# A triangular inverse whose diagonal blocks of 16 are solved row by row on VectorE, with packed gate products and folded square sums, in a one-core streaming-encoder layer

## The reference, cut to what matters

```python
L = jnp.where(strict, jnp.einsum('nbhtd,nbhsd->nbhts', kb, kc) * decay, 0.0)
T = lax.linalg.triangular_solve(L, eye, left_side=True, lower=True, unit_diagonal=True)
u = jnp.einsum('nbhts,nbhse->nbhte', T, vc * bc[..., None])
w = jnp.einsum('nbhts,nbhsd->nbhtd', T, kb * jnp.exp(G)[..., None])
```

```python
def rmsnorm(x, g):
    y = xf * lax.rsqrt(jnp.mean(xf * xf, axis=-1, keepdims=True) + EPS)
```

## Time and profile before

| | |
|---|---|
| time, median of 3 runs | 2031.48 us (2030.72 to 2032.32) |
| the profiled execution: its time, its span | 2031.48 us, 2029.6 us |
| granted clock of TensorE, mean | 0.998 |
| DVE, ACT, POOL busy | 1221.1 (60%), 898.0 (44%), 30.6 (2%) |
| DMA | 378.71 MB, mean 187 GB/s |

### The profile page before, as it was taken

The page is one execution under the profiler, slowest core; times in us unless marked ns, Lnnn a source line. Parts: engine busy times, 40 slices in busy tenths (PEclk is TensorE's granted clock), DMA queues, the critical chain, the costliest instruction groups (busy, mean ns, idle before and its releaser), DMA issues.

```text
span 2029.6 us, 35130 instructions
## 1 busy us (share of the span) xinstructions
PE 2014.8 (99%) x15008; PEld 1923.9 (95%) x15008; DVE 1221.1 (60%) x1330; ACT 898.0 (44%) x890; POOL 30.6 (2%) x53
## 2 busy tenths in 40 slices
PE   8999999999999999999999999999999999999999
PEld 8999999999999999999999999988888888888888
DVE  5677644544544467576564445778777777854444
ACT  5445333434365434454444434544444444433333
POOL 0000000000000000000000000000000000000000
PEclk9999999999999999999999999999999999999999
DMA  8565444555556856556565446655565656566664
GB/s 269 174 200 193 140 141 140 191 175 174 182 172 210 288 172 223 189 176 190 174 189 157 131 156 199 219 196 186 186 198 174 207 175 197 171 207 210 192 200 138
DMA packets 355454, 378.71 MB, mean 187 GB/s; under 512 B 8015, under 2 KB 351347, under 8 KB 353939
## 3 DMA queue, kind: packets, MB, share of 16 engines
q1 hardware_dynamic: 350947, 353.63, 54.7%
q0 software_dynamic: 4400, 23.48, 3.1%
HBM read 366.06 MB, written 11.02 MB: 186 GB/s over the span
## 4 chain that ended last, share of the span: by engine, by line
PE 97%; DMA 1%; DVE 1%; ACT 1%; issue 0%; SPq 0%; DVEq 0%; ACTq 0%
PE bank L1884 18%; PE bank L1885 18%; PE bank L1886 18%; PE bank L1921 16%; PE bank L1923 8%; PE bank L2395 8%; PE bank L2396 4%; PE bank L2078 1%; PE bank L2125 1%; DMA raw<-in_w_in 1%; PE bank L2303 1%; PE bank L2322 1%; DVE w_lo_home L1083 1%; ACT w_hi_home L496 0%; PE bank L2119 0%; PE bank L1989 0%
## 5 line engine op out<-in xcount | busy, mean ns | idle before, releaser
L1083 DVE TENSOR_TENSOR w_lo_home<-raw,w_hi_home 128x2048 fp32r<-128x2048 f32 (+1 forms) x349 | 756.8, 2169 | 602.4 <-ACT w_hi_home L496 602.0
L496 ACT ACTIVATE w_hi_home<-raw 128x2048 fp32r<-128x2048 f32 (+2 forms) x359 | 645.1, 1798 | 1071.6 <-PE bank L1886 639.3
L1884 PE MATMUL bank<-x_home,w_hi_home 128*128 128x256 f32 x2304 | 648.8, 282 | 2.2 <-DVE w_lo_home L1083 2.2
L1885 PE MATMUL bank<-x_home,w_hi_home 128*128 128x256 f32 x2304 | 643.6, 279 | 0.0
L1886 PE MATMUL bank<-x_home,w_lo_home 128*128 128x256 f32 x2304 | 642.9, 279 | 0.0
L1921 PE MATMUL bank<-x_home,w_hi_home 128*128 128x512 f32 x1408 | 488.5, 390 | 0.1
L1884 PEld LDWEIGHTS bank<-x_home,w_hi_home 128*128 128x128 f32 x2304 | 433.4, 188 | 3.0 <-issue 2.7
L1885 PEld LDWEIGHTS bank<-x_home,w_hi_home 128*128 128x128 f32 x2304 | 433.5, 188 | 0.2
L1886 PEld LDWEIGHTS bank<-x_home,w_lo_home 128*128 128x128 f32 x2304 | 433.2, 188 | 0.0
L1923 PE MATMUL bank<-x_home,w_lo_home 128*128 128x256 f32 x1408 | 397.0, 282 | 0.0
L1921 PEld LDWEIGHTS bank<-x_home,w_hi_home 128*128 128x128 f32 x1408 | 264.4, 188 | 55.7 <-issue 0.4
(11 more groups left out here) (301 smaller groups left out, 2003.7 us busy)
## 6 DMA issues: line engine op xcount, KB each, us to landing
raw<-in_w_in SPq DMA_DIRECT2D x52, 2048.0 KB, 8.7
raw<-in_ffn_up SPq DMA_DIRECT2D x44, 2048.0 KB, 8.0
raw<-in_ffn_down SPq DMA_DIRECT2D x32, 1408.0 KB, 6.5
raw<-in_xa_wkv SPq DMA_DIRECT2D x16, 2048.0 KB, 9.2
raw<-in_w_br SPq DMA_DIRECT2D x8, 2048.0 KB, 8.2
raw<-in_w_out SPq DMA_DIRECT2D x8, 2048.0 KB, 8.2
raw<-in_xa_wq SPq DMA_DIRECT2D x8, 2048.0 KB, 8.2
raw<-in_xa_wo SPq DMA_DIRECT2D x8, 2048.0 KB, 8.3
```

The costliest lines, as they stand in the source:

```text
L496: return nc.scalar.activation(out_, in_, func, **kw)
L1083: tt(split_out(w_lo, kind, half), halves(raw, kind, half, par), split_out(w_hi, kind, half).bitcast(f32), ALU.subtract).then_inc(lo_ready, 1)
L1884: mm(o, w[0], x[0], start=start, stop=False)
L1885: mm(o, w[0], x[1], start=False, stop=False)
```

## The change

Levels 0 to 3 of the ladder go. In their place the diagonal blocks of 16 (12 matrices with 8 blocks each, 96 blocks) are inverted by forward substitution on DVE, one block a partition. The 96 blocks come to 96 partitions through device memory: POOL stores all of `S_L`, loads the blocks of 16x16 into `block_l`, and when DVE has `block_v` (the inverses) and `block_u` (their transposes), stores these into zeroed copies of the 12 matrices, and loads the whole as `S_U` and `S_T`. The zeros are stored beforehand. PE runs h7 to h13 with nothing between, and then levels 4, 5 and 6.

The gates: the low part moves to the columns 16 above the high part in a second tile (`gw_both`), so that one product with `x_hi` gives both. ACT copies the sums to the SBUF (`gate_sums`), and one f32 matmul with `fold` adds the two rows of each gate. The norms: DVE adds the four strips down to one (`fold_squares`), and PE forms one f32 matmul, in the middle of the next half.

```diff
+LEVELS, FIRST_LEVEL = 7, 4
+BS = 1 << FIRST_LEVEL
+BLOCKS = 12 * P // BS
...
+        def diagonal_store(name):
+            step = BS * P + BS
+            flat = nc.dram_tensor(name, [BLOCKS * step], f32).ap()
+            whole = flat.rearrange("(n q) -> n q", n=12)[:, 0:P * P].rearrange("n (r c) -> r n c", r=P)
+            return whole, flat.rearrange("(b q) -> b q", b=BLOCKS)[:, 0:BS * P].rearrange("b (i c) -> b i c", i=BS)[:, :, 0:BS]
... POOL
-            pool.memset(gw_lo[:, :, :].bitcast(f32), 0.0).then_inc(gw_zero, 1)
+            pool.memset(S_U, 0.0).then_inc(gw_zero, 1)
+            pool.memset(gw_both[:, :, :].bitcast(f32), 0.0).then_inc(gw_zero, 1)
...
+            pool.wait_ge(gw_zero, 3)
+            pool.wait_ge(half_used, first_half("A", 4))
+            pool.dma_start(v_all, S_U).then_inc(rows, 16)
+            pool.wait_ge(half_used, first_half("A", 5))
+            pool.dma_start(u_all, S_U).then_inc(rows, 16)
...
-            for i in range(GA_UNITS - 1):
+            store_gates(0)
+            store_gates(1)
+            pool.wait_ge(l_v, 12)
+            pool.dma_start(l_all, S_L).then_inc(rows, 16)
+            store_gates(2)
+            pool.wait_ge(rows, 96)
+            pool.dma_start(square(block_l), l_diag).then_inc(rows, 16)
+            store_gates(3)
+            pool.wait_ge(c_v, BLOCK_OPS)
+            pool.dma_start(v_diag, square(block_v)).then_inc(rows, 16)
+            pool.dma_start(u_diag, square(block_u)).then_inc(rows, 16)
+            store_gates(4)
+            pool.wait_ge(rows, 144)
+            pool.wait_ge(half_used, first_half("GA", 6))
+            pool.dma_start(S_U, u_all).then_inc(rows, 16)
+            store_gates(5)
+            pool.wait_ge(rows, 160)
+            pool.wait_ge(half_used, first_half("GA", 7))
+            pool.dma_start(S_T, v_all).then_inc(rows, 16)
+            for i in range(6, GA_UNITS - 1):
                 store_gates(i)
... ACT
             for at, c0, k in GATES:
-                last = copy(gw_hi[:, :, at:at + k], gw[:, :, c0:c0 + k])
+                copy(gw_hi[:, :, at:at + k], gw[:, :, c0:c0 + k])
+                last = copy(gw_both[:, :, at:at + k], gw[:, :, c0:c0 + k])
             last.then_inc(gw_h, 1)
             for m in range(2, 7):
                 beside(m)
+                if m == 3:
+                    act.wait_ge(row_mm, 1)
+                    copy(gate_sums[:, :], bank[4][:, 0:SEQ]).then_inc(gw_h, 1)
... DVE
+            def fold_squares(k):
+
+                for i, n in ((3, 512), (4, 256)):
+                    dve.wait_ge(n_add, 5 * (k - 1) + i)
+                    tt(tmp[:, 0, 0:n], tmp[:, 0, 0:n], tmp[:, 0, n:2 * n], ALU.add).then_inc(n_add, 1)
...
-            cc(tt(S_C, S_L, bc(lev[:, 0, :].unsqueeze(1), bshape), ALU.mult))
+            cc(v.memset(block_v, 0.0))
             cc.settle()
-            cc(tt(S_T, bc(ident[:, :].unsqueeze(1), bshape), S_C, ALU.subtract))
+            cc(v.memset(block_v[:, 0:BS * BS:BS + 1], 1.0))
...
+            def forward_rows(js):
+
+                for j in js:
+                    n = BS - 1 - j
+                    below = block_p[:, 0:n * (j + 1)].rearrange("p (i c) -> p i c", i=n)
+                    cc.settle()
+                    cc(tt(below, bc(square(block_l)[:, j + 1:BS, j:j + 1], [BLOCKS, n, j + 1]),
+                          bc(square(block_v)[:, j:j + 1, 0:j + 1], [BLOCKS, n, j + 1]), ALU.mult))
+                    cc.settle()
+                    rows_v = square(block_v)[:, j + 1:BS, 0:j + 1]
+                    cc(tt(rows_v, rows_v, below, ALU.subtract))
...
                 elif l == 1:
+                    beside(m)
+                    dve.wait_ge(rows, 112)
+                    forward_rows(range(BS // 2 - 1))
+                    beside(m + 1)
+                    forward_rows(range(BS // 2 - 1, BS - 1))
+                    cc.settle()
+                    cc(v.tensor_copy(square(block_u), block_v.rearrange("p (i j) -> p j i", i=BS)))
+                elif l == 2:
                     kv(tt(tm[:, 0, 6:12, :], tm[:, 0, 6:12, :], bc(tail[:, 0:GH].unsqueeze(2), hs), ALU.mult))
                     dve.wait_ge(col_e, 3)
                     kv(tt(tm[:, 1, 6:12, :], tm[:, 1, 6:12, :], bc(beg.unsqueeze(2), hs), ALU.mult))
-                elif l == 2:
+                elif l == 3:
... PE
-                pe.wait_ge(n_add, 3 * k)
-                for j in range(4):
-                    last = mm(bank[3][:, 0:SEQ], ones[:, :], tmp[:, 0, j * SEQ:(j + 1) * SEQ], start=j == 0, stop=j == 3)
-                last.then_inc(n_ss, 1)
+                product_half(m + 3, acts, ks=range(KC // 2))
+                pe.wait_ge(n_add, 5 * k)
+                mm(bank[3][:, 0:SEQ], ones[:, :], tmp[:, 0, 0:SEQ], start=True, stop=True).then_inc(n_ss, 1)
+                product_half(m + 3, acts, ks=range(KC // 2, KC))
...
+                mm(bank[4][:, 0:SEQ], gw_both[:, k, :], x_hl[:, 0, k, :], start=k == 0, stop=False)
+                last = mm(bank[4][:, 0:SEQ], gw_hi[:, k, :], x_hl[:, 1, k, :], start=False, stop=k == KC - 1)
             last.then_inc(row_mm, 1)
-            for m in range(3, 14):
+            product_half(3)
+            pe.wait_ge(gw_h, 2)
+            mm(bank[4][:, SEQ:2 * SEQ], fold, gate_sums[:, :], start=True, stop=True).then_inc(row_mm, 1)
...
-            for l in range(7):
+            for _ in range(2 * FIRST_LEVEL - 1):
+                product_half(m)
+                m += 1
+            pe.wait_ge(rows, 160)
+            for l in range(FIRST_LEVEL, LEVELS):
...
+                if l == FIRST_LEVEL:
+                    pe.wait_ge(rows, 176)
```

More of the change, by code:

```diff
@@ L105, in shape_masks @@
     ident = (r == c)
-    levels = [((r >> (l + 1)) == (c >> (l + 1))) & ((r >> l) % 2 == 1) & ((c >> l) % 2 == 0) for l in range(7)]
+    levels = [((r >> (l + 1)) == (c >> (l + 1))) & ((r >> l) % 2 == 1) & ((c >> l) % 2 == 0) for l in range(FIRST_LEVEL, LEVELS)]
     upper = r <= c
@@ L480, in raw_bank @@
             return bank[(2 if a else 4) + c]
+        LOWER = 16
+        gate_sums, fold = rstd, cols[:, 0, :]
         GATES = ((0, 0, GH), (32, GH, GH), (64, 2 * GH, MH), (96, 2 * GH + MH, MH))
@@ L745, in _ @@
             m += 7
-            for l in range(7):
+            for l in range(LEVELS):
                 beside(m)
-                for g in range(3 if l else 0):
+                for g in range(3 if l >= FIRST_LEVEL else 0):
                     act.wait_ge(z_t, level_start(l) + g + 1)
-                    if l > 1 and g == 0:
-                        act.wait_ge(d_t, 3 * (l - 1))
+                    if l > FIRST_LEVEL and g == 0:
+                        act.wait_ge(d_t, 3 * (l - FIRST_LEVEL))
                     copy(S_Z[:, 4 * g:4 * g + 4, :].rearrange("p c s -> p (c s)"), bank[5 + g][:, :]).then_inc(z_e, 1)
-                for g in range(3 if l > 1 else 0):
+                for g in range(3 if l > FIRST_LEVEL else 0):
                     act.wait_ge(z_t, level_start(l) + 3 + g + 1)
@@ L1250, in _ @@
             for at, c0, k in GATES:
-                last = tt(gw_lo[:, :, at:at + k], gw[:, :, c0:c0 + k], gw_hi[:, :, at:at + k].bitcast(f32), ALU.subtract)
-            last.then_inc(gw_l, 1)
+                tt(gw_both[:, :, at + LOWER:at + LOWER + k], gw[:, :, c0:c0 + k], gw_hi[:, :, at:at + k].bitcast(f32), ALU.subtract)
+            pairs = lambda s: s.rearrange("p (g x i) -> p g x i", g=4, x=2)
+            v.tensor_copy(pairs(fold)[:, :, 1, :], pairs(ident[:, :])[:, :, 1, :])
+            tt(pairs(fold)[:, :, 0, :], pairs(ident[:, :])[:, :, 0, :], pairs(ident[:, :])[:, :, 1, :], ALU.add).then_inc(gw_l, 1)
             for m in range(2, 6):
@@ L1380, in _ @@
             beside(m + 3)
-            dve.wait_ge(rows, 48)
+            dve.wait_ge(rows, 80)
             for h in range(GH):
@@ L1434, in _ @@
                     v.scalar_tensor_tensor(t, o, -1.0, t, ALU.mult, ALU.add).then_inc(d_e, 1)
-                beside(m + 1 if l else m)
+                if l != 1:
+                    beside(m + 1 if l else m)
                 m += 2 if l else 1
@@ L1506, in _ @@
             dve.wait_ge(mask_in, 32)
-            dve.wait_ge(rows, 64)
+            dve.wait_ge(rows, 192)
             beside(m)
@@ L1972, in norm_beside @@
                 product_half(m + 2, acts)
[L1973 to L1977 removed]
+                product_half(m + 3, acts, ks=range(KC // 2))
+                pe.wait_ge(n_add, 5 * k)
+                mm(bank[3][:, 0:SEQ], ones[:, :], tmp[:, 0, 0:SEQ], start=True, stop=True).then_inc(n_ss, 1)
+                product_half(m + 3, acts, ks=range(KC // 2, KC))
+                for j in range(4, 8):
                     product_half(m + j, acts)
@@ L2041, in _ @@
             for k in range(KC):
-                last = three(bank[4][:, 0:SEQ], [t[:, k, :] for t in (gw_hi, gw_lo)], [x_hl[:, j, k, :] for j in range(2)],
-                             k == 0, k == KC - 1)
```

(22 more changed lines are left out.)

75 lines of the change are left out of this document (32 added, 43 removed).

## The result

The changed kernel took 2003.66 us, the median of 4 runs (2002.98 to 2004.39). The kernel before took 2031.9 us (4 runs, 2030.72 to 2033.03). The ratio is 0.9861, with an interval from 0.9849 to 0.9873. The profiled execution of the changed kernel took 2002.98 us with a span of 2001.0 us, 28.5 us less than that of the kernel before.

What follows compares the result with a forecast made beforehand. PE was taken as the bound, busy 2014.8 of 2029.6 us. Ladder, gates, norms and a new wait summed as 2031.48-21.3-1.3-2.5+1.4 = 2007.8 us, with a range of 2005.5 to 2012.5 us.

Steps and rivals of the forecast that it cites:

- What bounds the kernel: Whole kernel: PE's program alone makes the time in ladder, gates and norms; each instruction removed returns its distance to the next.
- The ladder on PE: Levels 0 to 3 removed and level 4 without transposes: 21.3 us less on PE; levels 5 and 6 untouched.
- The forward substitution on DVE: Block inverse: parts of 3.3 and 3.8 us, 5.9 with copy and scalings; PE waits 1.4 us before h11.
- The gates and the norms: Gate products and sums of squares on PE: 1.3 us net saved at the gates, 2.5 us at the norms.
- The transfers: Block loads and stores through device memory and weights loads: all in time, cost nothing, at most 1 us.
- Slow stores: Rival at the 64-byte block stores: at twice 50.6 ns a piece PE waits 7.8 us, 2015.6 us; chance 0.09.
- slow steps: Rival in the forward substitution: 0.40 us a step, waits of 6.2 us in place of 1.4, 2012.6 us; chance 0.08.
- the chain of transfers: Rival, slower than before: the inverse's 9216 transfer pieces in series; at 8 ns each waits 36.8 us, time 2043; chance 0.03.
- the one from below: Lower bound for forward substitution steps on DVE: 0.17 us an operation, giving a PE wait of 0.2 us.
- The sum: Whole kernel: the profiled execution's 2031.48 us less the savings plus the 1.4 us wait gives 2007.8 us.
- The range: Whole kernel: 2005.5 to 2012.5 us, low end for smaller waits, high end for slow steps and part of slow stores.
- still a little below: Outcome for the whole kernel: a time a little under the forecast's 2006.4 to 2009.5 us; chance 0.02.

Runs made afterwards that it cites:

- e3: The changed kernel with the two scalings behind the forward substitution moved behind the next `lo`; 2002.45 us, ratio 0.9861 to the kernel before.
- e4: The kernel before with its four loads of stored merge gates issued one to three halves later; 2034.33 us, ratio 1.0016.
- e5: The changed kernel with the four loads of stored merge gates issued one to three halves later; 2009.01 us, ratio 0.9895 to the kernel before.
- before_again: The kernel before, unchanged, run once more for a second profile; 2034.16 us in one run.
- before_third: The kernel before, unchanged, run for a third profile; 2033.65 us.
- e7: The kernel before with the second to fourth loads of stored merge gates one half later; 2034.04 us, ratio 1.0012.
- e6: The changed kernel with merge-gate loads one to three halves later and the two scalings behind the next `lo`; 2006.77 us, ratio 0.9882 to the kernel before.
- e2: The kernel before with only the packed gates and folded norms, its ladder of seven levels kept; 2024.75 us, ratio 0.9968; second profile 2024.92 us.

## Why the prediction was right and where it was wrong

- **What bounds the kernel** was right. With no wait of PE in the places of the change, each PE instruction that went gave back its distance to the next.
- **The ladder on PE**, 21.3 us, was right: e3, which has no wait there, gains 21.23.
- **The forward substitution on DVE**: 3.3, 3.8 and 5.9 us, measured 3.3, 3.8 and 5.84. The wait before h11 was 1.24 us where 1.4 stood, and 0.9 by the lengths alone. The chain of dependent 8-element operations was the right row to take, and runs of 96 partitions with broadcast operands cost nothing extra.
- **The gates and the norms**, 1.3 and 2.5 us, were mis-sized by one number: an f32 matmul alone was priced by the distance of eight in a row (2 records of 0.206 us), and it holds the stream for 0.24 us. That is 0.17 us at the gates (1.5 measured) and 2 x 0.17 at the norms, 2.8. The trace has 3.0; the rest is twice the 0.09 us by which the group of eight stood further behind the product ahead of it (0.21 against 0.12).
- **The transfers**: cost nothing, right. PE waits for no `slab`. POOL's issues grow to 1.0 us, and PE waits for none of them.
- **The rivals** fell. Slow stores need a wait of PE at level 4, which is not there; slow steps need 0.40 us each, and they are 0.17 to 0.22 us long; the chain of transfers is in time. Of the bounds for the steps, the one from below was 0.1 us too small: at 0.17 us a step the prediction's own terms give a wait of 0.3 us, not 0.2.
- **The sum** is the step that failed. "The sum for the profiled execution is 2031.48-21.3-1.3-2.5+1.4 = 2007.8 us" takes all the rest of that execution over unchanged. Two of its stretches are not fixed. It began with 1.4 us of long low clock, as no other profile did at its start, and it had the late load near 661 us, with the 1.6 us of PE that stood in the earlier trace rows as the longest wait for `lo`. I read that row as smallness ("2.2 us in three places") and did not ask whether a kernel whose program is 24 us further at that place would wait there at all. I also priced a load by the median landing, 8.7 us, where this one took 15.0. What the runs showed in place of an unchanged rest is a gain of 1.7 us at the start, 1.8 at the late load and 0.95 in the plain halves, 4.4 us in all. Every profile of the kernel before has the late load and none of the changed one has it. Between the profiles of e4 and e5, where it is in neither, the change measures 24.5 us.
- **The range** followed from that. Its low end, 2.3 us below the forecast, held only smaller waits in the ladder, and "still a little below" had 0.02. The 1.6 us of the late load, by the earlier trace rows, and the 0.5 of the lone f32 matmuls come to 2.1 us, nearly the whole of that distance, with nothing left for the start.

Of the extra 4.4 us, then, 1.8 are the late load, shown by repeated profiles though not explained; 1.7 are the start, chance for the most part; 0.95 differ from one execution to the next. That the profiled pair, 28.5 us apart, agrees with the medians is partly luck, since no other profile has its long dip at the start. In medians the terms, 24.3, leave 3.5 to 3.9 of the 27.8 and 28.2 us. The late load alone costs 1.8 us with the full clock and up to 4.0 with the fallen one, so it may account for half of that or for all. In how many of the runs without a kept trace the clock fell there is not on record, and how much is left for the start and the plain halves stays open.

## What to carry to other kernels

Where PE is the bound and never waits, count its starts: 21 of the 24 us came out within 0.1 us from the seven starts of the earlier trace rows. But look once more at each wait of PE anywhere in the program, near the edit or not: a transfer that is late by a few microseconds where two queues share the DMA engines can come in time, or later still, in a changed kernel, so its wait belongs into the range in both directions. And it can cost more than its length: in before_again the granted clock fell behind a wait of 2.2 us, and the place cost 4.0. Do not let a `lo` queue behind work that nobody waits for: moving two scalings gave 1.4 us in the traces, 1.1 to 1.2 in the medians.

## What the runs showed of the hardware

- An f32 matmul of 256 columns, recorded twice, costs the stream 0.24 us alone between rounded products, and a row of eight records 0.206 us each. The row of eight also starts 0.21 us behind the product ahead of it, the lone one 0.12; in both cases the product behind takes another 0.19 us.
- A dependent VectorE operation on 96 partitions is 0.17 us long at 15 elements and 0.22 at 63, and the next starts 0.03 us behind its end. The formula of the Trainium skill (VectorE: DVE Perf Modes, the section on the TRN2 errata) gives 173 and 223 ns, with which the trace agrees.
- POOL takes 1.0 us to issue a transfer of 1536 pieces, and 0.55 us for one of 128 rows.
- Two executions of the same program are 1.4 us apart at 34 us, with a low-clock stretch at the start of 7 us in the one and of some 3 us in the other.
- TensorE's clock fell to 1.2 GHz behind some waits of PE in mid-stream and not behind others, and the length of the wait does not sort them: it fell behind 2.1 and 2.2 us (before_third, before_again, for 3.4 us), 3.6 (e4, 3.4 us) and 3.3 (e7, 6.8 us), and not behind 1.6 (the kernel before), 2.7 and 2.6 (e5, e6).
- A load of 2048 KB beside which two pieces of 1152 KB are loaded landed 15.0 to 15.7 us behind its issue in the kernel before, 11.0 in the changed one, and 12.2 and 13.5 in e2, with nearly the same distances between the issues.
- Runs of halves start 5.65 us apart in place of 5.60 at a granted clock of 1.00, at places that differ between executions of the same program, and cost up to 1.7 us in an execution.
